# Differential attention: the mix of two maps goes from GpSimd to VectorE, with the first map's weight

## What is computed

```
def probs(qb, kf):
    s = einsum('bhqd,bhkd->bhqk', qb, kf) * scale + bias
    s = where(causal, s, -inf)
    return softmax(s, axis=-1)

p = probs(qb1, k1f) - lamf * probs(qb2, k2f)
out = einsum('bhqk,bhkd->bhqd', p, vf)
```

## Time and profile before

| | |
|---|---|
| median of 3 runs | 3345.98 us (3337.95 to 3349.73) |
| profiled execution | 3353.64 us, span 3351.9 us |
| TensorE busy | 2962.7 us, 88% |
| VectorE busy | 1561.5 us, 47% |
| ScalarE busy | 1235.2 us, 37% |
| GpSimd busy | 736.0 us, 22% |

### The profile page before, as it was taken

The page is one execution under the profiler, slowest core; times in us unless marked ns, Lnnn a source line. Parts: engine busy times, 40 slices in busy tenths (PEclk is TensorE's granted clock), DMA queues, the critical chain, the costliest instruction groups (busy, mean ns, idle before and its releaser), DMA issues. The chain is left out here.

```text
span 3351.9 us, 34912 instructions
## 1 busy us (share of the span) xinstructions
PE 2962.7 (88%) x13448; PEld 2385.1 (71%) x13448; DVE 1561.5 (47%) x1927; ACT 1235.2 (37%) x2024; POOL 736.0 (22%) x323
## 2 busy tenths in 40 slices
PE   6999998877778989988998999694889989998998
PEld 5787887666667767776777778482677877787786
DVE  3666552346764337777878777514322111121121
ACT  3455442334542335555554554423224111111110
POOL 2111111100002322332233323112223212121111
PEclk7999999989989989999999999897999999999999
DMA  4111122131224212121112212241330111111112
GB/s 112 44 45 57 53 68 76 30 63 40 57 79 158 84 55 68 46 65 50 54 46 65 63 53 82 106 131 58 126 126 26 44 44 38 50 50 38 44 44 76
DMA packets 239270, 218.90 MB, mean 65 GB/s; under 512 B 29304, under 2 KB 200856, under 8 KB 239128
## 3 DMA queue, kind: packets, MB, share of 16 engines
q1 hardware_dynamic: 238096, 215.41, 21.0%
q10 hardware_dynamic: 1032, 1.57, 0.3%
HBM read 156.66 MB, written 41.42 MB: 59 GB/s over the span
## 5 line engine op out<-in xcount | busy, mean ns | idle before, releaser
L179 POOL TENSOR_TENSOR w_lo<-w_raw,w_hi 128x1024 fp32r<-128x1024 f32 (+3 forms) x220 | 521.1, 2371 | 2014.1 <-ACT w_hi L171 2014.1
L171 ACT ACTIVATE w_hi<-w_raw 128x1024 fp32r<-128x1024 f32 (+3 forms) x220 | 215.3, 983 | 666.5 <-PE u_y_ps L1688 221.3
L209 PE MATMUL d_pp<-h_hi,w_hi 128*128 128x512 f32 x896 | 367.9, 411 | 32.5 <-DVE d_padded L2523 20.7
L2501 DVE SCALAR_TENSOR_TENSOR d_acc<-d_padded,vectors,d_acc 128x1024 f32<-128x1024 f32 x240 | 388.3, 1618 | 3.6
L209 PE MATMUL d_pp<-h_hi,w_lo 128*128 128x512 f32 x896 | 366.2, 409 | 0.0
L209 PE MATMUL d_pp<-h_lo,w_hi 128*128 128x512 f32 x896 | 363.4, 406 | 0.0
L209 PEld LDWEIGHTS d_pp<-h_hi,w_hi 128*128 128x128 f32 x896 | 173.2, 193 | 80.2 <-issue 25.4
L209 PE MATMUL s_pp<-h_hi,w_hi 128*128 128x512 f32 x512 | 206.8, 404 | 13.1 <-PEq L67 13.1
L2281 POOL TENSOR_TENSOR d_probs<-d_probs 128x128 f32<-128x128 f32 (+3 forms) x64 | 129.5, 2024 | 385.8 <-ACT d_probs L2397 385.8
L209 PE MATMUL s_pp<-h_hi,w_lo 128*128 128x512 f32 x512 | 205.2, 401 | 0.0
L209 PE MATMUL s_pp<-h_lo,w_hi 128*128 128x512 f32 x512 | 204.2, 399 | 0.0
(11 more groups left out here) (346 smaller groups left out, 6542.7 us busy)
## 6 DMA issues: line engine op xcount, KB each, us to landing
w_raw<-in_w_in SPq DMA_DIRECT2D x97, 512.0 KB, 3.8
w_raw<-in_w_gate_up SPq DMA_DIRECT2D x44, 512.0 KB, 3.8
w_raw<-in_w_down SPq DMA_DIRECT2D x22, 512.0 KB, 3.7
gates<-s_gate SPq DMA_DIRECT2D x16, 512.0 KB, 5.1
f_gate<-gates SPq DMA_DIRECT2D x16, 512.0 KB, 4.8
w_raw<-in_w_out SPq DMA_DIRECT2D x16, 512.0 KB, 3.9
w_raw<-in_w_proj SPq DMA_DIRECT2D x16, 512.0 KB, 4.8
x_tok_in<-in_x SPq DMA_DIRECT2D x8, 512.0 KB, 9.0
```

What stands on the lines that cost most here:

```text
L171: act.activation(self.hi[:, s, 0:chunks, :], self.raw[:, s, 0:chunks, :], ACT.Copy).then_inc(self.rounded[s], 1)
L179: pool.tensor_tensor(self.lo[:, s, 0:chunks, :], self.raw[:, s, 0:chunks, :], f32(self.hi[:, s, 0:chunks, :]), ALU.subtract).then_inc(self ...
L209: mm = pe.matmul(halves(ps)[h], w[:, k, :], x[:, k, h * HALF:(h + 1) * HALF], start=(k == 0 and r == 0), stop=(k == chunks - 1 and r == 2))
L2501: dve.scalar_tensor_tensor(out=acc[:, :], in0=x, scalar=wt, in1=acc[:, :], op0=ALU.mult, op1=ALU.add).then_inc(c["taps"], 1)
```

## The change

`mix` leaves GpSimd and becomes one VectorE instruction, that multiplies map 1 by its weight and adds map 2. ScalarE weighs map 2 alone; `scaled` counts one per step instead of two. VectorE waits for that count before the mix; `top` waits for `mixed` of two steps ago, an instruction of its own engine, where it waited for `scaled`. GpSimd keeps the low parts of the weight tiles.

```diff
         @block.gpsimd
         def _(pool):
-            def mix(s):
-
-                n = (s % QB + 1) * P
-                pool.wait_ge(c["scaled"], 2 * s + 2)
-                pool.tensor_tensor(probs[:, s % 2, 0:n], probs[:, s % 2, 0:n], probs[:, 2, 0:n],
-                                   ALU.add).then_inc(c["mixed"], 1)
-
...
-                    if x == 0:
-                        mix(s)
             ring.subtract_ahead(pool)
...
             def weigh(s):
                 n = (s % QB + 1) * P
                 act.wait_ge(c["weighted"], 2 * s + 2)
-                for a in range(2):
-                    p = probs[:, (s % 2, 2)[a], 0:n]
-                    act.activation(p, p, ACT.Copy, scale=stats[:, 2 * (s % 2) + a, 3:4]).then_inc(c["scaled"], 1)
+                act.activation(probs[:, 2, 0:n], probs[:, 2, 0:n], ACT.Copy,
+                               scale=stats[:, 2 * (s % 2) + 1, 3:4]).then_inc(c["scaled"], 1)
...
                 if s >= 2:
-                    dve.wait_ge(c["scaled"], 2 * (s - 1))
+                    dve.wait_ge(c["mixed"], s - 1)
...
+            def mix(s):
+                n = (s % QB + 1) * P
+                dve.wait_ge(c["scaled"], s + 1)
+                dve.scalar_tensor_tensor(out=probs[:, s % 2, 0:n], in0=probs[:, s % 2, 0:n],
+                                         scalar=stats[:, 2 * (s % 2), 3:4], in1=probs[:, 2, 0:n], op0=ALU.mult,
+                                         op1=ALU.add).then_inc(c["mixed"], 1)
...
                     taps(PARTS * s + x, False)
+                    if x == 0 and s < STEPS:
+                        mix(s)
             normalise("o", LAST)
```

## The result

| | before | after |
|---|---|---|
| median | 3348.61 us (8 runs, 3337.95 to 3352.78) | 3363.92 us (8 runs, 3362.41 to 3368.28) |
| ratio to before, 95% interval | | 1.0052 (1.0040 to 1.0063) |
| profiled execution | 3353.64 us, span 3351.9 | 3367.19 us, span 3365.4 |
| stage, first to last transpose of the weights | 854.0 us | 867.1 us |
| one head (head 3 to 4) | 109.8 us | 112.7 us |

The change makes the kernel slower by 15 us. The spans of the two profiled executions differ by 13.5 and their stages by 13.1, so all but 0.4 of it lies in this stage. "One head" is here the time from VectorE's normalisation of q in one head to that in the next. The ratio is near that of the mean times, not of the medians; the two can differ by some 0.0006.

A forecast was written before the change was run, and what follows sets the result against it. TensorE was taken to bound the stage, VectorE second. Heads 0 to 4 +7.4, half clock +8.5, heads 5 and 6 -1.3, last head -1 sum to +13.6, say +13: 3359 us, range 3331 to 3374.

The forecast's parts named there:

- TensorE's pace and VectorE as second limit: Differential stage, 932 us: TensorE, busy 852, sets the pace with 80 us of holes; where VectorE is late, TensorE stops.
- b=3 to b=5, -0.67, -0.3, -0.3: Blocks of 128 queries numbered 3 to 5 in a head: shorter scaling, then fewer blocked taps, save these us.
- b=6, +1.5: Query block 6 of a head: GpSimd's low part of the weights gets in before a tap, delaying the next maximum 1.5 us.
- b=7, +1.25: Query block 7 of a head: the mix delays VectorE's low part of three blocks by 1.25 us.
- The hole, 4.1 us, with half clock behind: TensorE before the transposes at the head's change: its wait grows from 1.37 to 4.1 us, with clock 0.5 behind it.
- One more half-clock stretch per head: Behind the head's change: TensorE at the lower clock for 3.4 us loses 1.7 us, +8.5 for five heads.
- Heads 5 and 6, -1.3: Heads with more tiles and no hole at their end: only the shorter scaling at b=3 counts, -1.3 us together.
- The taps, 40 of 80 us recovered: VectorE's taps: some 40 of 80 us excess, caused by GpSimd's mixes, goes; the other 40, from low parts, stays.
- The mix blocked like a tap in b=5: Query block 5 of a head: GpSimd's low part of the weights blocks VectorE's new mix for 0.7 us.
- the collisions just go: Rival, chance 0.20: low parts land where VectorE reads PSUM, so heads end earlier; -16 us, 3330.
- Full: Rival, chance 0.13: VectorE's gaps take no mix, so wide mixes lie on the path; +27 us, 3373.
- TensorE hides it: Rival, chance 0.22: gains at b=3 to 5 and losses at b=6, 7 cancel, no further clock stretch; within 5 us, 3346.

## Why the prediction was right, and where it was not

The sign, the size (+15 measured, +13 put on the median) and the way there held; some terms of the sum did not. That the stage came out within 0.5 us of the sum (13.1 against 13.6) is partly luck: heads 0 to 4 gave 13.5 where 15.9 were put, heads 5 and 6 gave +0.4 where -1.3 was put, and the last head -0.7 where -1 was put, so two errors of about 2 us cancel.

1. **TensorE's pace and VectorE as second limit:** right. TensorE's busy time is the same, and the loss is in its waits for d_t_lo and d_padded.
2. **b=3 to b=5, -0.67, -0.3, -0.3:** the marks give -0.57, -0.15, -0.51. Right in sum.
3. **b=6, +1.5:** +1.44 from mark to mark. The tap at 3.08 us is the sign that the forecast named, and holding the low part back gave back 1.81.
4. **b=7, +1.25:** from the first tap to the low part of three blocks it is 7.04 us (1824.54 to 1831.58) against 5.87 (1813.74 to 1819.61), +1.2.
5. **The hole, 4.1 us, with half clock behind:** 3.73 and 3.27, with 0.53 and 0.51. Taking away that clock alone gave 1.5 a head. That at d_padded is 3.12, not near 2.7, since TensorE comes to it without the half clock ahead of it.
6. **One more half-clock stretch per head:** right where it counts, wrong as a count. Ahead of the last transposes both stages have the same time at the lower level, 51 us, and heads 0 to 4 one stretch more, not five. The stretch behind the hole of b=5 mostly went and the one at the head's change came. They aren't worth the same. In the earlier trace rows the one at 1775 is followed by the hole at d_padded, so that TensorE, late or not, waits for VectorE (2.99 with it, 1.02 and 3.12 without). Behind the head's change nothing later absorbs it: until the normalisation VectorE waits for TensorE. Head 2 of the kernel before had such a loss already (a hole of 3.04 us at b=6 with half clock behind it), which the prediction, reading one pattern for heads 1 to 4, did not have; it fits with that head growing by 0.9 only.
7. **Heads 5 and 6, -1.3:** wrong, +0.4. I took only b=3 for them, but the collision of b=6 is there too: the maximum of b=7 comes 1.4 and 1.9 later after the normalisation of q than before. Their other work hides most of it. The last head gave 0.7 instead of 1: the wait for the last mix went (2.34), and one of 1.67 for the low part took its place.
8. **The taps, 40 of 80 us recovered:** the worst-sized term, 14. The half that I counted is there: in head 4 the mixes' blocking of 1.2 us at b=4 and 2.0 each at b=5 and b=7 is gone, 5 us a head. But the sum over all taps left the low parts' harm as it was, and they now fall on taps in two places more. At b=2 a tap takes 3.44 us (1755.78), where in the kernel before the low part hit no tap (it slowed the normalisation behind, 2.10 us instead of 1.27), and at b=6 one takes 3.08 (1814.57): 4 us a head given back. Those at b=1, b=4 (4.63 us for two at 1775.87, as before) and b=7 (4.74 for two) stay. It didn't spoil the sum, because that went by place and had both: the one of b=2, of no cost to the end of the head, and the one of b=6.
9. **The mix blocked like a tap in b=5:** 1.53 us at 1797.98, where widths 640 and 896 give 0.885 and 1.152: 0.5 of waiting against the 0.7 put. This is the rule cited from the Trainium skill, SBUF — State Buffer, "Who interferes with whom"; this trace agrees with it for the new instruction as well.
10. **Mixes, 52 us in all:** 56.3; blocking of the width of 768 is 3.5 of the difference.

Of the rivals, "the collisions just go" failed at the step that it was warned of: the low part of b=6 does get in. But half of it can be had: held back by one wait the kernel is level with before, and with the taps behind the low part as well it is 0.25% faster. "Full" needs a late scaling, which the kernel with both scalings showed (31 us more by the medians). "TensorE hides it" was right up to the maximum of b=7 (+0.2 us) and failed behind it, where the low part of three blocks and the half clock bring 2.7 us a head. That ScalarE's saving without the move would be the better change wasn't tried.

## What to carry to other kernels

Price an instruction that changes engines by where it lands in the order there, and ask of every engine that is relieved what it now starts earlier and what that meets; totals of busy time allowed -28 to +72 us here, the sum along one head's chain came within 2 us, some of it by errors that cancelled. A hole of TensorE and the half clock behind it cost only if no later wait would absorb them, so follow each to the next wait before removing or adding one. Idle time ahead of an instruction is not slack of those that stand before it, unless none of them is on the path to what it waits for.

## What was not expected of the hardware

- A hole of nearly the same length is followed by half clock in one case and not in another: 3.21 us with 0.51 behind it in the kernel before, 3.23 with 1.00 in the kernel after, at the same instruction. What TensorE did ahead of them differs, and no run here was made to separate that.
- Two delays that each open the same hole don't add up: either taken away alone brings 16 or 18 us of stage back, since the clock's 8 us hang on the hole that both make. Taken away together they bring 23.
- What GpSimd's low part and VectorE's multiply-add cost each other hangs on which started first and how long it still has to run. In b=6 after, the low part (3.12 us against 2.36 free) first waited out a tap, and the next tap (3.08 against 1.27) then waited out the low part. In b=6 before, the low part took 3.46 and the tap its 1.27. The mix of b=5 after met only the end of a low part and lost 0.5.
